# Sample tile's self-attention output product as two rounded products with split weights

## What is computed

```
y = concat(y_a, y_b) @ w_out        # y_a: pooling (layer 0) or convolution (layer 1), 512 channels
x = x + y                           # y_b: self-attention heads, 512 channels; w_out is 1024 x 1024
x = x + cross_attention(rmsnorm(x, norm_cross))
x = x + ffn(rmsnorm(x, norm_ffn))   # layer 0: dense SwiGLU; layer 1: top 2 of 8 experts
```

## Time and profile before

| What | Value |
| --- | --- |
| Device time, median of 3 runs | 1919.95 us (1916.07 to 1920.38) |
| The profiled execution, its own time | 1921.69 us |
| Its span | 1919.9 us |
| PE busy | 1813.6 us (94%) |
| DVE busy | 1270.1 us (66%) |
| ACT busy | 1065.5 us (56%) |
| POOL busy | 170.8 us (9%) |
| Mean granted clock of PE | 0.97 |
| HBM traffic over the span | 259 GB/s |

### The profile page before, as it was taken

How to read it: one execution, slowest core, us unless ns; L and a number is a source line. 1 busy time by engine, 2 the same in 40 slices (tenths; PEclk the granted TensorE clock), 3 DMA queues, 4 the chain that set the end, 5 groups by cost and what they waited for, 6 DMA issues and landing times.

```text
span 1919.9 us, 23758 instructions
## 1 busy us (share of the span) xinstructions
PE 1813.6 (94%) x8733; PEld 1423.0 (74%) x8733; DVE 1270.1 (66%) x1223; ACT 1065.5 (56%) x1054; POOL 170.8 (9%) x169
## 2 busy tenths in 40 slices
PE   7988998999998977998899999999999999999997
PEld 6676444999997965445588888888888788888884
DVE  5544133544436774223689888898888888889895
ACT  4333123332315446313577877778787777777672
POOL 4220010000002840010100000000000000000010
PEclk8989999999998987999799999999999999999999
DMA  9442326644435532426499999999999999999993
GB/s 307 160 154 67 121 72 224 193 136 140 144 121 176 206 127 67 128 82 225 174 382 378 373 393 364 393 372 381 389 364 397 365 374 389 364 395 369 387 385 134
DMA packets 236753, 497.88 MB, mean 259 GB/s; under 512 B 15010, under 2 KB 46898, under 8 KB 236669
## 3 DMA queue, kind: packets, MB, share of 16 engines
q1 hardware_dynamic: 223645, 479.11, 69.4%
q0 software_dynamic: 4544, 13.57, 2.0%
q10 hardware_dynamic: 8496, 4.33, 0.8%
HBM read 480.46 MB, written 17.35 MB: 259 GB/s over the span
## 4 chain that ended last, share of the span: by engine, by line
PE 53%; DMA 2%; DVE 2%; ACT 1%; issue 0%; POOL 0%; DVEq 0%; SPq 0%; POOLq 0%
PE bank L1159 45%; PE bank L555 3%; DMA big<-in_we_down 1%; PE bank L1218 1%; DMA small_ring<-in_we_down 1%; PE bank L1179 0%; DVE big_r L2994 0%; PE bank L1169 0%; PE bank L545 0%; PE bank L1196 0%; PE bank L650 0%; ACT big_r L1737 0%; ACT small_ring_r L1737 0%; PE bank L943 0%; PE bank L922 0%
## 5 line engine op out<-in xcount | busy, mean ns | idle before, releaser
L1737 ACT ACTIVATE big_r<-small_ring 128x2048 fp32r<-128x2048 f32 x240 | 456.2, 1915 | 140.0 <-DMA small_ring<-in_we_up 46.6
L2994 DVE TENSOR_TENSOR small_ring_r<-small_ring,big_r 128x2048 fp32r<-128x2048 f32 x192 | 436.9, 2289 | 36.8 <-ACT big_r L1737 36.1
L1159 PE MATMUL bank<-big_r,hT_r 128*128 128x512 f32 x1024 | 384.7, 393 | 1.6 <-DVE kM_r L3000 1.6
L1159 PE MATMUL bank<-small_ring_r,hT_r 128*128 128x512 f32 x768 | 301.4, 392 | 0.0
L1159 PE MATMUL bank<-big_r,kM_r 128*128 128x512 f32 x704 | 274.8, 390 | 0.0
L2994 DVE TENSOR_TENSOR big_r<-big,small_ring_r 128x2048 fp32r<-128x2048 f32 x96 | 219.4, 2291 | 39.5 <-ACT small_ring_r L1737 39.5
L1159 PEld LDWEIGHTS bank<-big_r,hT_r 128*128 128x128 f32 x1024 | 192.6, 188 | 41.3 <-issue 1.8
L1737 ACT ACTIVATE small_ring_r<-big 128x2048 fp32r<-128x2048 f32 x96 | 183.4, 1916 | 51.2 <-DMA big<-in_we_up 27.3
L1159 PEld LDWEIGHTS bank<-small_ring_r,hT_r 128*128 128x128 f32 x768 | 144.6, 188 | 30.0
L1159 PEld LDWEIGHTS bank<-big_r,kM_r 128*128 128x128 f32 x704 | 132.8, 189 | 26.8
L1737 ACT ACTIVATE big_r<-big 128x2048 fp32r<-128x2048 f32 x59 | 113.2, 1919 | 42.2 <-DMA big<-in_we_down 13.1
(11 more groups left out here) (407 smaller groups left out, 2978.8 us busy)
## 6 DMA issues: line engine op xcount, KB each, us to landing
small_ring<-in_we_gate SPq DMA_DIRECT2D x80, 1024.0 KB, 5.9
small_ring<-in_we_up SPq DMA_DIRECT2D x64, 1024.0 KB, 5.6
big<-in_we_down SPq DMA_DIRECT2D x64, 1024.0 KB, 5.8
big<-in_we_up SPq DMA_DIRECT2D x48, 1024.0 KB, 6.6
small_ring<-in_we_down SPq DMA_DIRECT2D x48, 1024.0 KB, 5.7
big<-in_we_gate SPq DMA_DIRECT2D x32, 1024.0 KB, 5.3
small_ring<-in_w_gate SPq DMA_DIRECT2D x11, 1024.0 KB, 5.4
small_ring<-in_w_up SPq DMA_DIRECT2D x11, 1024.0 KB, 7.9
```

The lines of the kernel that those rows point to most:

```text
L1159: ins = mm(dst, x_hi_lo[xa][kk], wcols, start=(m < 2 or j == 0) and kk == 0 and (xa, wa) == (0, 0), stop=(m < 2 or j == STAGES - 1) and kk ...
L1737: return A(out, in_, ACT.Copy)
L2994: V.tensor_tensor(low[i % PRING], raw[i % PRING], high[i % PRING].bitcast(F32), ALU.subtract) \
```

## The change

In `out_projection` the call of `out_tile(l, 2, hf)` is replaced by 16 rounded (fp32r) matmuls: for each of the 8 chunks one with 128 stationary columns (the samples' high and low parts side by side) and the high weights, and one with 64 stationary columns (the high part) and the low weights. PSUM rows 0 to 63 hold the high parts' product, rows 64 to 127 that of the low parts; both are added to x. To feed this:

- ACT copies four weight pieces of 128x2048 to `wo_hi` (over the key and query buffers of the self-attention) in `sample_out(l, 1)`, between the copies of PT and `osam`, and the samples' high columns in two halves (`sample_high`); after each half product it copies the low rows to `wo_low`.
- DVE makes four low weight pieces (`wo_lo`) in place in the ring slot, so each half's only after prompt tile 1's product has read it, and two low token pieces (`sample_lo`), in `attention_residuals(l, 1)`. `residual_sample` adds twice where `residual` added once.
- POOL clears `qbd` after `norm_power` of the three tiles instead of before it, since `wo_hi` uses that space.

```diff
@@ out_projection (PE)
-                    out_tile(l, 2, hf)
+                    b = open_bank("wo", l, hf, 2)
+                    for q in range(2):
+                        if hf == 0:
+                            pe.wait_ge(*at("x_hi", "wo", l, q))
+                            pe.wait_ge(*at("w_lo", "wo_tokens", l, q))
+                        pe.wait_ge(*at("w_hi", "wo", l, hf, q))
+                        pe.wait_ge(*at("w_lo", "wo", l, hf, q))
...
+                            for low_part in ((True, False) if c == KD - 1 else (False, True)):
+                                if low_part:
+                                    ins = mm(bank[b][0:NSAMP, :], sample_hl[:, c, 0, :], w[1][:, k, :], start=False, stop=False)
+                                else:
+                                    ins = mm(bank[b][:, :], both, w[0][:, k, :], start=c == 0, stop=c == KD - 1)
+                    ins.then_inc(full[b], 1)
@@ POOL
+                norm_power(3 * l + 1)
                 nc.gpsimd.memset(qbd[:, 0:2048], 0.0).then_inc(*sets("qbd0", 2 * l + 1))
-                norm_power(3 * l + 1)
@@ sample_out (ACT), between the copies of PT and of osam
+                if hf:
+                    take("ss", l, 3)
+                    for half in range(2):
...
+                        for q in range(2):
+                            copy(wo_hi[half][q], raw_piece(key, q)).then_inc(*sets("w_hi", "wo", l, half, q))
+                    sample_high(l, 0)
@@ after the self-attention (ACT), layer 1 alike
             forget_attention()
+            sample_high(0, 1)
             norm_squares(1, (1,))
-            to_hT(1, range(2))
+            for hf in range(2):
+                to_hT(1, (hf,))
+                wo_low_out(0, hf)
@@ attention_residuals(l, 1) (DVE)
                     residual("wo", l, 3 * l + 1, 0, 1)
                     residual("wo", l, 3 * l + 1, 1, 0)
+                    sample_lo(l, 0)
+                    wo_lo(l, 0, 0)
+                    wo_lo(l, 0, 1)
                     norm(3 * l + 1, (0,))
                     residual("wo", l, 3 * l + 1, 1, 1)
+                    sample_lo(l, 1)
+                    wo_lo(l, 1, 0)
                     norm(3 * l + 1, (1,))
+                    wo_lo(l, 1, 1)
@@ residual_sample (DVE), in place of residual("wo", l, 3 * l + 1, 2, hf)
+                b = take("wo", l, hf, 2)
+                dve.wait_ge(*at("x_hi", "wo_low", l, hf))
+                xs = x[0:NSAMP, 2, hf * HALF:(hf + 1) * HALF]
+                V.tensor_tensor(xs, xs, bank[b][0:NSAMP, :], ALU.add).then_inc(free[b], 1)
+                dve.wait_ge(*taken("wo", l, hf, 2))
+                V.tensor_tensor(xs, xs, wo_low[hf][0:NSAMP], ALU.add).then_inc(*sets("w_lo", "wo_sum", l, hf))
```

More of the change, by code:

```diff
@@ L335, in decoder_step @@
         HI_SLOTS = (("ck", "cv", "q", "k", "v", "p"), ("ck", "g", "a", "cv", "q", "k", "v"))
+        wo_hi = [[big_r[:, o_ + q * PIECE:o_ + (q + 1) * PIECE] for q in range(2)] for o_ in (0, 8192)]
+        sample_hl = big_r[:, 14336:14336 + KD * 2 * NSAMP].rearrange("p (c h t) -> p c h t", c=KD, h=2)
+        wo_low = [big[:, 15360 + HALF * hf:15360 + HALF * (hf + 1)] for hf in range(2)]
         moe_x = [t[:, 0:1024].rearrange("p (k c) -> p k c", k=KD) for t in (hT_r, rounded("kM"))]
@@ L848, in out_projection @@
                     tokens_to_channels(3 * l + 1, hf)
-                    out_tile(l, 2, hf)
+                    b = open_bank("wo", l, hf, 2)
[5 more added lines that the diff above has]
+                        pe.wait_ge(*at("w_lo", "wo", l, hf, q))
+                        w = [p_.rearrange("p (k n) -> p k n", k=KD // 2) for p_ in (wo_hi[hf][q], lo_piece(("wo", l, hf), q))]
+                        for k in range(KD // 2):
+                            c = q * (KD // 2) + k
+                            both = sample_hl[:, c, :, :].rearrange("p h t -> p (h t)")
+                            for low_part in ((True, False) if c == KD - 1 else (False, True)):
[4 more added lines that the diff above has]
+                    ins.then_inc(full[b], 1)
                     release(("wo", l, hf), "wo", l, hf, 2)
@@ L1868, in ahead, with sample_high, wo_low_out @@
                     keys_out(stage, 1, AHEAD[i])
+            def sample_high(l, q):
+                if q:
+                    for g in (2, 3):
+                        act.wait_ge(*taken("ost", l, g))
+                elif l == 0:
+                    act.wait_ge(*taken("pm", NCH - 1))
+                else:
+                    act.wait_ge(*at("y_mix", NCH - 1))
+                copy(sample_hl[:, 4 * q:4 * q + 4, 0, :], yT[:, 4 * q:4 * q + 4, SEQ:T]).then_inc(*sets("x_hi", "wo", l, q))
+            def wo_low_out(l, hf):
+                b = take("wo", l, hf, 2)
+                copy(wo_low[hf][0:NSAMP], bank[b][NSAMP:2 * NSAMP, :]).then_inc(*sets("x_hi", "wo_low", l, hf))
             def sample_out(l, hf):
@@ L1876, in sample_out @@
                 ahead(2 * l, hf, 1)
+                if hf:
+                    take("ss", l, 3)
+                    for half in range(2):
+                        key = ("wo", l, half)
+                        slot, n = slot_of(key)
+                        act.wait_ge(slot_full[slot], 16 * n)
+                        for q in range(2):
+                            copy(wo_hi[half][q], raw_piece(key, q)).then_inc(*sets("w_hi", "wo", l, half, q))
+                    sample_high(l, 0)
                 for g in gs:
@@ L2221, in _ @@
             stick_attention()
+            sample_high(1, 1)
             norm_squares(4, (1,))
-            to_hT(4, range(2))
+            for hf in range(2):
+                to_hT(4, (hf,))
+                wo_low_out(1, hf)
             norm_squares(4, (2,))
@@ L2439, in residual, with wo_lo, sample_lo, residual_sample @@
                     dve.sem_inc(*sets("x", j, t))
+            def wo_lo(l, half, q):
+                key = ("wo", l, half)
+                dve.wait_ge(*at("w_hi", *key, q))
+                V.tensor_tensor(lo_piece(key, q), raw_piece(key, q), wo_hi[half][q].bitcast(F32), ALU.subtract) \
+                    .then_inc(*sets("w_lo", *key, q))
+            def sample_lo(l, q):
+                dve.wait_ge(*at("x_hi", "wo", l, q))
+                cs = slice(4 * q, 4 * q + 4)
+                V.tensor_tensor(sample_hl[:, cs, 1, :], yT[:, cs, SEQ:T], sample_hl[:, cs, 0, :].bitcast(F32), ALU.subtract) \
+                    .then_inc(*sets("w_lo", "wo_tokens", l, q))
+            def residual_sample(l, hf):
+                j = 3 * l + 1
+                b = take("wo", l, hf, 2)
+                dve.wait_ge(*at("x_hi", "wo_low", l, hf))
[3 more added lines that the diff above has]
+                V.tensor_tensor(xs, xs, wo_low[hf][0:NSAMP], ALU.add).then_inc(*sets("w_lo", "wo_sum", l, hf))
+                if hf:
+                    dve.wait_ge(*at("w_lo", "wo_sum", l, 0))
+                    dve.wait_ge(*at("w_lo", "wo_sum", l, 1))
+                    dve.sem_inc(*sets("x", j, 2))
             def attention_residuals(l, hf):
@@ L2730, in _ @@
                 to_hT(1, (hf,))
-                residual("wo", 0, 1, 2, hf)
+                residual_sample(0, hf)
             norm(1, (2,))
@@ L2882, in _ @@
                 to_hT(4, (hf,))
-                residual("wo", 1, 4, 2, hf)
+                residual_sample(1, hf)
             norm(4, (2,))
```

## The result

The changed kernel takes 1904.5 us (median of 5 runs, 1900.7 to 1905.1), the kernel before 1917.5 (5 runs). The ratio is 0.9923 with a 95% interval of 0.9909 to 0.9936: faster by 0.77%, or 14.8 us, between 12.3 and 17.5; the two medians lie 13.0 us apart. The forecast was 10.5 us, a ratio of 0.9945. The direction was right, and in this comparison the size was too small by more than the measurement's uncertainty.

The account below looks back on a forecast made before the run. PE was taken to bound the stretch: 6.7 us saved a layer, less 1.2 for norm 1 and 0.2 for DVE's queue, gives 5.25, twice 10.5. From the median 1919.95 that forecast 1909.5 us, range 1904 to 1915.

Parts of the forecast that it names:

- PE is the bound there, a shorter product pays in full: Sample tile's output product: PE never waits in 15.02 us a layer, and nothing behind, experts included, swallows the gain.
- Each half 3.65 us, pair 0.46: Each fp32 half product of 7.0 us becomes eight matmul pairs, 3.65 us, from the FFN's pair of 0.46 us.
- ACT costs nothing, cover 1.1 us: ACT's four high weight pieces and first sample copy end about 224.2, 1.1 us before the osam copy at 225.33.
- POOL's collision, 1.5 us, and a stall of 1.2 us: Before norm 1, DVE's low piece holds POOL's small instruction 1.5 us longer, so PE idles 1.2 us a layer.
- The hand-over costs 0.2 us and DVE's queue sets it: Start of cross attention: DVE's queued copies and adds make tile 1's hT ready at 246.75, costing PE 0.2 us.
- The moved clearing costs nothing: POOL's clearing of qbd, now beside norm 2, charged nothing; charged in full, 0.1 us a layer.
- Full gain: Rival: POOL doesn't collide, PE never waits at norm 1; 6.4 us a layer, 1907.1 us; chance 0.18.
- The clock rival: Rival: PE's 1.2 us idle gap lowers its clock once a layer, losing 6.9 of 10.5 us; 1916.4; chance 0.09.
- Slower: Rival: PE's clock falls and stays low through cross attention's first three products, 21 us longer; 1930.5; chance 0.04.
- Experts swallow it: Rival: loads, not PE, pace the last 970 us and start no earlier, leaving no gain; 1919.95; chance 0.05.
- pairs no faster: Rival: rounded pairs run no faster than fp32, leaving only new waits of 1.4 us a layer; 1922.8; chance 0.02.
- Both layers have the same rows, so 2 x 5.25 = 10.5 us: Sum: cross attention starts 5.25 us earlier in each layer, taken as the whole kernel's gain of 10.5 us.

Follow-up runs that it names:

- the piece cut short: Changed kernel, DVE's low piece for half 1's first four chunks subtracted over 64 of 2048 columns, PE using high weights instead; stretch 9.43 us for 10.82, no ratio.
- the kernel with the norm first: Changed kernel with DVE's norm of tile 1 ahead of the low piece for half 1's first chunks; stretch 11.63 us for 10.82, no ratio.
- the transposes on ACT: Changed kernel, half 1's first four chunks ahead of tile 1's transposes, ACT making all four hT copies of tiles 0 and 1; ratio 0.9919 to the kernel before.
- two kernels that arrived 9 us apart: The kernel before, and the same with the sample tile's output products over 4 of 8 chunks; dense FFN to layer 1 took 482.4 and 482.6 us.

## Why the prediction was right or wrong

- *PE is the bound there, a shorter product pays in full.* Right: 10.46 us of the gain are the two stretches, and in the first pair of profiles the experts keep their 975.2 us.
- *Each half 3.65 us, pair 0.46.* The pairs are 0.46 us apart, but the first of a half takes 0.55, so that a half takes 3.8 us (232.86 to 236.41, and 0.23 for the last matmul). The transposes ahead are left sooner, 0.80 and 0.85 us for 1.03. Together with the wait (1.34 for 1.2) and the hand-over (below) these errors cancel to less than 0.1 us a layer. That the sum for the stretch is right to 0.1 us is in part luck.
- *ACT costs nothing, cover 1.1 us.* Right, cover 1.66. I had charged four separate copies; in a row they overlap, each takes 1.91 us and the next starts 1.80 behind, 7.31 us for 7.66.
- *POOL's collision, 1.5 us, and a stall of 1.2 us.* Right: 1.58 us instead of 0.19, a stall of 1.17 by the bracket, and with the piece cut short both vanish. This was read off one row near the start of the kernel, in a stage that has nothing to do with the change.
- *The hand-over costs 0.2 us and DVE's queue sets it.* Right. DVE's last copy ended at 242.63 and the cross attention started 0.25 us behind it, as it did in the kernel with the norm first (248.27 and 248.51), where the bracket names that copy. Without that wait it would have started 0.23 us behind the last matmul's start of 242.36, as it does with the transposes on ACT (243.91 and 244.14). So the hand-over cost 0.29 us.
- *The moved clearing costs nothing.* Right, by its own run.
- *The rivals.* "Full gain" did not happen locally. The clock rival had the right engine and the wrong place: the pause of 1.17 us lowered nothing (granted clock 1.00 in the stretch). The falls again and again of which the Trainium skill tells (TensorE: Matmul & The Clock Gate, "HAM oscillation — how this bites in real kernels") did not follow here; the waits in that section's kernel are longer than this pause. "Slower" fell with it. "Experts swallow it" and "pairs no faster" fell with the table.
- **The step that failed** is the silent assumption in "Both layers have the same rows, so 2 x 5.25 = 10.5 us" that all else shifts unchanged. I took the granted clock as a risk behind the stretch, with a price only upward. By the means of three profiles of each kernel, the stretches give 10.5 us, and three later parts do not keep their length: 0.4 us longer ahead of the dense FFN, 2.6 shorter behind its start, 1.7 longer in layer 1's cross attention. That makes 11.0. The 2.6 came with the length of the stretch in every profile; the 1.7 came in two of three.
- *The rest is open.* The spans differ by 14.2 us in the mean. The remaining 3.2 lie in parts that differ between executions of one kernel: 2.1 ahead of any changed instruction (230.1 to 236.6 us in the changed kernel, 232.3 to 236.7 before) and 1.2 in the experts (972.4 to 975.2 in the changed kernel, 972.2 to 977.7 over all kernels). The ratios 0.9923, 0.9945 and 0.9917 mean 13.8 us, with intervals of some 3 to 4 us to either side. Whether the gain beyond 11 us is chance or belongs to the change is not shown.
- *The range* held the median, 1904.5 against its lower end of 1904, but the ratio on its own base, 1902.7, lies under it. Its lower end took in the bounds of the stretch and the spread of the runs one at a time; their sum, 1906.5 less 3.9, is 1902.6. No gain from the clock was in it.

## What to carry to other kernels

Before you give DVE a long subtraction with two SBUF inputs, look for the small POOL instruction that will fall under it and for who waits for that; the price may already stand in another stage's rows. Count the engine that prepares the operands as a queue with a fixed start: here DVE's two in-place pieces can't begin before the last reader of the raw weights. Moving the norm in that queue lost 0.8 us; giving PE other work under the wait and two copies to ACT won 0.7. In a kernel with stages in which PE idles often, compare the changed stretch by its own borders in the trace, and treat the rest as a term of its own, of either sign, even if its code is untouched.

## What the runs showed of the hardware

- The clock lost in a later stage can depend on position: two kernels that arrived 9 us apart had the same granted clock to 0.01 in the windows shown, and the changed kernel took 2.6 us less for the same code in three of three profiles, though by two different patterns.
- The granted clock at the start of a busy stage decides its pace: 59 instructions of PE in 10 us at 0.85, 51 at 0.73, with 4 us of work in the 10 us ahead in both.
- In plain fp32, a product with 128 stationary columns started 0.87 us behind the start of eight transposes, one with 64 columns 1.03 us (0.80 for the rounded pair); that the columns are the reason is not shown.
- DVE's subtraction of 2.29 us held a POOL instruction of 0.19 us to its end (1.58 and 1.76 us); POOL's clearing of 1.79 us and a DVE norm of 1.28 us ran side by side at their usual length, while in its old place the clearing had held a scaling of 0.39 us, which took 1.97.
